# A hybrid encoder layer with product-key retrieval: half of the tokens' input projections moved from ahead of the gather loop into its slots 104 to 200

## The chip, the core and the metric

The kernel runs on one core of a Trainium2 chip. The metric is the device time of one execution in microseconds (us). The five engines are TensorE (PE), VectorE (DVE), ScalarE (ACT), GpSimd (POOL) and SyncE (SP); each works through its own list of instructions in order, and they meet through semaphores.

## The reference, cut to what matters

One layer for 512 prompt tokens and 32 sample tokens, D = 1024, everything in float32:

```
n    = rmsnorm(x)
proj = n @ w_in                      # qkv (3072), z, x_lru, y_lru, gate_a, gate_b (1024 each), beta, decay (16)
A    = gated DeltaNet(conv4+silu(qkv)), gated by silu(z)        # sequential over tokens, in chunks
B    = RG-LRU(conv4(x_lru)) * gelu(y_lru)                        # sequential over tokens
x    = x + (sigmoid(gate_a)*(A @ w_branch_a) + sigmoid(gate_b)*(B @ w_branch_b)) @ w_out
q    = rmsnorm(x) @ w_q;  8 heads x top-16 of 128x128 product keys -> 128 experts a token
x    = x + sum_k gelu(u_k . n) * gate_k * v_k                     # u, v: rows of two 16384 x 1024 tables
y    = rmsnorm(x)
```

The convolutions and both recurrences carry state from token to token, so later tokens need three rows of history and one hidden state from the earlier ones. The states and the last three pre-convolution rows are outputs too.

## The kernel before, in words

**Tokens and tiles.** Four prompt tiles of 128 tokens and a sample tile of 32. In the projections tokens lie along the free axis (544 columns, in two halves of 272) and features along the partitions. From the delta rule on, the work goes tile by tile.

**The front part.** `w_in` and `w_branch_b` arrive as 72 chunks of 128 output columns (512 KB each) in a ring of four buffers, in the order lx, ly, ga, gb, branch_b, z (8 each), qkv (24). Each chunk is split in two: ACT casts it to the rounded type fp32r (`split`, L919, into one of only two buffers `w_hi`), POOL subtracts to get the remainder (`lower`, L1190). The inputs were split likewise. PE (`quads`, L601) then runs hi x hi, lo x hi and hi x lo over 8 blocks of 128 and two column halves: 48 one-pass matmuls of 272 columns a chunk. ACT empties the banks (`evac` L888 to L894, or `through` L966) and then casts the chunk after the next one, which can't start before PE has left that `w_hi` buffer. DVE does the convolutions (`conv`, L1259 and L1263) and the LRU (L1277 to L1293); ACT its tanh, exp and square root (L983 to L991). The gates of the LRU are 16 small products (L638). What tiles 1 to 3 need later is written to DRAM (`spill`, 18 transfers) and read back a tile at a time (`loads`).

**The trunk.** For each tile `delta` (two groups of four heads, one stage apart) and `tail` (products with w_a, w_out, w_q and the keys, one 512 KB weight chunk to a stage, ordinary float32 matmuls) are generators that name the stage of each step. `BD` and `BT` hold the first stage of each tile's delta and tail: 47 stages (35 for a full tile's solve, 12 more) and 36. `Weave.to(stage)` emits all steps up to a stage into an engine's list, and every engine and SP use the same stages.

**The gather loop.** There are 544 slots, one expert per token row each: a slot fetches 128 rows of 8 KB (u and v side by side, 1.05 MB) by an indirect DMA (POOL, L1211) into a ring of 8 slot buffers. DVE forms the dot with u (`dot`, L1541), ACT its gelu once per pair of slots (L1170), DVE the share (L1550), ACT a diagonal matrix (L1156), and PE adds share times v to the token's sum in two PSUM banks (`add_row`, L863), three slots later (VLAG). POOL may fetch into a buffer again when PE has used it (`slot_free`). Between slots each engine does its share of the trunk: `stage_at` gives the stage reached at each slot, from a table:

```
PACE = [(2, 92, BD[1], BD[2]), (92, 220, BD[2], BD[3]), (220, 348, BD[3], stages)]
```

So tile 1's delta and tail lie in slots 2 to 92, tile 2's in 92 to 220, tile 3's and the sample tile's in 220 to 348; the rest has gathers alone. Tile 0's delta and tail come ahead of the loop. Tile t's slots begin at 128 t, and the picks of the experts (`pick_halves`, `pick_top`, `pick_experts` on DVE, one for 16 slots) run LAG = 2 blocks ahead.

## Time and profile before

| | us |
|---|---|
| runs (median of 3) | 2364.37 (2353.43 to 2369.49) |
| profiled execution, its own time | 2363.84 |
| its span, first to last instruction | 2361.7 |
| front part, first to last L601 matmul | 49.3 to 533.0 |
| delta and tail of tile 0, first pick | 533.0 to 702.4 |
| first dot of the gather loop | 711.7 |
| last dot | 2345.2 |
| mean granted TensorE clock | 0.948 |

The page gives each engine's busy time; a view by windows gives it for any stretch, with the granted clock (1.00 is 2.4 GHz, 0.50 is 1.2 GHz) and the DMA share. Dots leave two records each (the operation and the read of its accumulator), float32 matmuls two as well. Recorded times of PE overlap, so that the distance from start to start is what one costs.

### The profile page before, as it was taken

How to read it: one execution, taken by the hardware profiler on the slowest of the kernel's cores; microseconds unless marked ns; L12 is line 12 of the kernel's file. 1: busy time of each engine (PE TensorE's matmuls, PEld its weight loads, DVE VectorE, ACT ScalarE, POOL GpSimd, SP SyncE). 2: the span in 40 equal slices, each digit the busy share in tenths (PEclk: the TensorE clock that was granted, in tenths of full speed). 3: DMA queues.
4: the chain of work that ended last, by engine and by line, in shares of the span. 5: the costliest groups of instructions: out<-in, count | busy, mean ns of one | idle time of the engine just before them, and what ended most of it. 6: DMA issues, size and time to landing. Idle time of an engine off the chain costs nothing.

```text
span 2361.7 us, 26994 instructions
## 1 busy us (share of the span) xinstructions
PE 2028.3 (86%) x9678; PEld 1331.2 (56%) x9678; DVE 1432.4 (61%) x3375; ACT 710.1 (30%) x1768; POOL 815.7 (35%) x631
## 2 busy tenths in 40 slices
PE   5999799998867998999988889998999777777776
PEld 5988799997745654555554456654536222322321
DVE  2603802775238974678865658868646667676754
ACT  3454223443114240352341233352312122221221
POOL 3423334440003333334333333334222434444442
PEclk6999899997888999999999999999999999999999
DMA  3212223422368999999999998999889999999997
GB/s 114 90 62 71 91 87 112 146 91 76 111 218 324 349 366 418 413 379 364 390 383 419 406 400 309 356 334 396 345 322 363 385 387 412 401 418 397 381 401 295
DMA packets 129642, 695.82 MB, mean 295 GB/s; under 512 B 14608, under 2 KB 33456, under 8 KB 59136
## 3 DMA queue, kind: packets, MB, share of 16 engines
q0 software_dynamic: 78416, 570.57, 61.6%
q1 hardware_dynamic: 50496, 121.69, 14.6%
q10 hardware_dynamic: 624, 2.23, 0.2%
q8 instruction: 57, 0.93, 0.2%
q14 instruction: 49, 0.40, 0.0%
HBM read 680.31 MB, written 13.61 MB: 294 GB/s over the span
## 4 chain that ended last, share of the span: by engine, by line
PE 45%; DMA 23%; DVE 17%; issue 8%; ACT 3%; POOL 3%; SPq 1%; DVEq 0%; POOLq 0%; ACTq 0%
DMA arena<-in_uv,arena 19%; PE ps L863 18%; PE ps L601 12%; DVE arena L1541 6%; PE ps L784 4%; PE ps L808 2%; DMA arena<-in_w_out 2%; DMA arena<-in_w_a 2%; POOL w_lo L1190 2%; PE ps L735 1%; PE ps L734 1%; PE ps L725 1%; DVE i L1478 1%; ACT arena L1156 1%; DVE v L1475 1%
## 5 line engine op out<-in xcount | busy, mean ns | idle before, releaser
L863 PE MATMUL ps<-arena 128*128 128x512 f32 (+1 forms) x2176 | 1052.8, 622 | 222.2 <-ACT arena L1156 220.6
L1211 POOL DMA_INDIRECT arena<-in_uv,arena x544 | 611.7, 1125 | 1190.9 <-PE ps L863 987.9
L1541 DVE CUSTOM_DVE_ANT_0 arena<-arena 128x1024 f32<-128x1024 f32 x544 | 662.2, 1223 | 426.5 <-DMA arena<-in_uv,arena 420.8
L863 PEld LDWEIGHTS ps<-arena 128*128 128x128 f32 (+1 forms) x2176 | 390.8, 192 | 723.6 <-issue 392.2
L1170 ACT ACTIVATE gelu_d<-dots 128x2 f32<-128x2 f32 x272 | 55.4, 204 | 1057.7 <-DVE dots L1541 1050.5
L601 PE MATMUL ps<-n_hi,w_hi 128*128 128x272 f32 x1024 | 298.5, 292 | 8.2 <-POOL w_lo L1190 8.2
L601 PE MATMUL ps<-n_hi,w_lo 128*128 128x272 f32 x1024 | 299.4, 292 | 0.0
L601 PE MATMUL ps<-n_lo,w_hi 128*128 128x272 f32 x1024 | 297.4, 290 | 0.0
L1190 POOL TENSOR_TENSOR w_lo<-arena,w_hi 128x1024 fp32r<-128x1024 f32 x72 | 188.4, 2617 | 298.4 <-ACT w_hi L919 298.3
L601 PEld LDWEIGHTS ps<-n_hi,w_hi 128*128 128x128 f32 x1024 | 195.9, 191 | 9.0 <-issue 8.1
L601 PEld LDWEIGHTS ps<-n_lo,w_hi 128*128 128x128 f32 x1024 | 196.1, 191 | 0.0
L601 PEld LDWEIGHTS ps<-n_hi,w_lo 128*128 128x128 f32 x1024 | 195.4, 191 | 0.0
L1156 ACT ACTIVATE arena<-ident,share 128x128 f32<-128x128 f32 x512 | 173.6, 386 | 0.3
L784 PEld LDWEIGHTS ps<-arena 128*128 128x128 f32 x1024 | 135.0, 202 | 36.5 <-issue 21.0
L784 PE MATMUL ps<-arena 128*128 128x128 f32 (+1 forms) x1024 | 137.1, 292 | 10.2 <-DMA arena<-in_w_a 8.2
L1263 DVE SCALAR_TENSOR_TENSOR arena<-arena,dn_w 128x547 f32<-128x547 f32 x72 | 98.6, 1370 | 10.4 <-DVE arena L1259 0.2
L919 ACT CAST w_hi<-arena 128x1024 fp32r<-128x1024 f32 x72 | 76.1, 1058 | 53.7 <-PE ps L601 53.7
L735 PE MATMUL ps<-arena 128*128 128x128 f32 (+1 forms) x448 | 75.5, 265 | 0.0
L725 PEld LDWEIGHTS ps<-arena 128*128 128x128 f32 (+1 forms) x448 | 54.3, 187 | 33.8 <-issue 24.6
L808 PE MATMUL ps<-arena 128*128 128x512 f32 x128 | 65.8, 633 | 8.4 <-DMA arena<-in_w_out 8.1
L1170 ACT ACT_TABLE_LOAD x54 | 69.3, 1283 | 1.0
L734 PE MATMUL ps<-arena 128*128 128x128 f32 (+1 forms) x368 | 66.3, 267 | 0.0
(232 smaller groups left out, 2127.7 us busy)
## 6 DMA issues: line engine op xcount, KB each, us to landing
arena<-in_stream SPq DMA_DIRECT2D x72, 512.0 KB, 3.3
arena<-in_w_a SPq DMA_DIRECT2D x32, 512.0 KB
arena<-in_w_out SPq DMA_DIRECT2D x32, 512.0 KB
arena<-in_w_q SPq DMA_DIRECT2D x32, 512.0 KB
arena<-in_uv,arena POOLq DMA_INDIRECT x544
spill<-arena SPq DMA_DIRECT2D x12, 512.0 KB, 5.8
arena<-spill SPq DMA_DIRECT2D x4, 1536.0 KB, 11.6
spill<-arena SPq DMA_DIRECT2D x6, 640.0 KB, 7.5
```

Source lines behind the costliest of these rows:

```text
L601: mm = pe.matmul(ps[:, b + half, 0:HALF], w[:, k, :], rhs[:, k, cols], start=(k == 0 and w is w_hi[s % 2] and rhs is rhs_hi), stop=(k == K ...
L734: pe.matmul(bank(PA)[:, i, 0:L], tinvt[0:L, h, 0:L], pmat[0:L, h, 0:L], start=True, stop=True)
L735: mm = pe.matmul(bank(PC)[:, i, 0:L], pmat[0:L, h, 0:L], tinvt[0:L, h, 0:L], start=True, stop=True)
L784: mm = pe.matmul(ps[:, bank + j, at:at + N], w[:, k, :], rhs[:, k, 0:N], start=(k == 0), stop=(k == KC - 1))
L808: mm = pe.matmul(ps[:, 5 + half, :], mix[:, k, 0:P], w[:, cols], start=(k == 0), stop=(k == KC - 1))
L863: mm = pe.matmul(ps[0:L, half, :], diag[k % NDIAG][:, 0:L], ring[k % SLOTS][:, D + half * 512:D + (half + 1) * 512], start=False, stop=k % ...
L1156: act.activation(diag[k % NDIAG][:, 0:L], eye, ACT.Identity, scale=share[u % 4][:, k % 2:k % 2 + 1]).then_inc(diag_ready, 1)
L1170: act.activation(gelu_d[u % 4][:, :], dots[u % 4][:, :], ACT.Gelu).then_inc(gelu_ready, 1)
L1190: pool.tensor_tensor(w_lo[s][:, :, :], wring[s], w_hi[s % 2][:, :, :].bitcast(F32), ALU.subtract).then_inc(lo_ready, 1)
L1211: pool.indirect_dma_start(out=ring[kk % SLOTS], out_offset=None, in_=a["uv"], in_offset=bass.IndirectOffsetOnAxis(ap=idx[:, kk:kk + 1], ax ...
L1263: ins = dve.scalar_tensor_tensor(out=y[:, 0:CONVW], in0=x[:, k:k + CONVW], scalar=w[:, k:k + 1], in1=y[:, 0:CONVW], op0=ALU.mult, op1=ALU.add)
L1541: ins = dve.tensor_tensor_reduce(ring[s][:, 0:D], ring[s][:, 0:D], n2p if t == NTILE else n2[t % 2], 1.0, 0.0, ALU.mult, ALU.add, dots[k / ...
```

## The change

Tiles 0 and 1 (N1 = 256 columns) are projected up front, the other N2 = 288 tokens inside the gather loop. The normalised input of those goes to DRAM (`spill_n`) and comes back at slot 104 as `NG`, 294 columns wide (3 + 256 + 3 + 32: room for the history).

- **Up front**: still 72 chunks, each with 24 matmuls of 256 columns into one bank (four banks in rotation in place of two pairs). Convolutions, LRU, gates and activations on 256 columns; results go straight to tiles 0 and 1 in SBUF, so the 18 spills and the loads for tiles 1 and 2 are gone. The parameter of the first normalisation and the first four chunks are issued ahead of the other parameters.
- **In the loop**: two new generators, `second_sums` and `second_lru`, of 87 stages from BG on. The same 72 chunks and the two LRU gate matrices are read again (74 transfers of 512 KB, through the four `wslot` buffers that the tails use), and multiplied in ordinary float32 with 294 columns (branch_b 288), rotating over six banks; then history columns written into PSUM by ACT, convolutions by DVE straight from PSUM, the LRU for 288 tokens, activations into tile 2's place, and for tile 3 and the samples through three staging buffers (`stg`) to `spill3` by 48 transfers of 80 KB.
- **Pace**: tile 1 in slots 1 to 104, the second projections in 104 to 200, tile 2 in 200 to 239, tile 3 and samples in 239 to 367. LAG is 1 and a block's picks lie at its slots 1, 4 and 7 (before 3, 7, 11).
- **Every second expert in slots 104 to 238** (odd, and not in the first 11 of a tile: 62 of them) is added by DVE into `fin` with one 128x1024 operation; PE and the diagonal matrix on ACT are left out for it. At a tile's end DVE adds the two sums (`join`).

```diff
-        PICK_AT = (3, 7, 11)
-        LAG = 2
+        PICK_AT = (1, 4, 7)
+        LAG = 1
+        def on_dve(k):
+            return 104 <= k < 239 and k % P > 10 and k % 2 == 1
...
+            if u == 2:
+                BG = stages
+                stages += 87
+                feed += [("stream", CH_LX + n, BG + n) for n in range(KC)]
+                feed += [("gate", j, BG + 17) for j in range(2)]
+                for first, at in ((CH_GA, 18), (CH_Z, 26), (CH_LY, 34)):
+                    feed += [("stream", first + n, BG + at + n) for n in range(KC)]
+                for n in range(KC):
+                    feed += [("stream", CH_GB + n, BG + 44 + 2 * n), ("stream", CH_BB + n, BG + 45 + 2 * n)]
+                feed += [("stream", CH_QKV + m, BG + 60 + m) for m in range(3 * KC)]
...
-        PACE = [(2, 92, BD[1], BD[2]), (92, 220, BD[2], BD[3]), (220, 348, BD[3], stages)]
+        PACE = [(1, 104, BD[1], BG), (104, 200, BG, BD[2]), (200, 239, BD[2], BD[3]), (239, 367, BD[3], stages)]
...
 # PE, front part
-                        for half in range(2):
-                            cols = slice(half * HALF, (half + 1) * HALF)
-                            for k in range(KC):
-                                for w, rhs in ((w_hi[s % 2], rhs_hi), (w_hi[s % 2], rhs_lo), (w_lo[s], rhs_hi)):
-                                    mm = pe.matmul(ps[:, b + half, 0:HALF], w[:, k, :], rhs[:, k, cols],
+                        for k in range(KC):
+                            for w, rhs in ((w_hi[s % 2], rhs_hi), (w_hi[s % 2], rhs_lo), (w_lo[s], rhs_hi)):
+                                mm = pe.matmul(ps[:, s, 0:N1], w[:, k, :], rhs[:, k, :],
...
 # PE, in the loop
+            def second_sums():
+                def product(p, i, rhs, n):
+                    c = group_at(i)
+                    w = wslot[c % RING].rearrange("p (k n) -> p k n", n=P)
+                    pe.wait_ge(chunk_in[c % RING], landed(c))
+                    if p >= 6:
+                        pe.wait_ge(*freed(p - 6))
+                    for k in range(KC):
+                        mm = pe.matmul(ps[:, group_bank(p), 0:n], w[:, k, :], rhs[:, k, :],
+                                       start=(k == 0), stop=(k == KC - 1))
+                    mm.then_inc(tw_used, 1)
...
 # SP
+                yield BG
+                sp.wait_ge(sc_copied, 2)
+                sp.wait_ge(n_spilled, 16)
+                sp.dma_start(NG[:, :, HIST:HIST + N1], a["spill_n"][:, :, 0:N1]).then_inc(ng_in, 16)
+                sp.dma_start(NG[:, :, SMP0:NP2], a["spill_n"][:, :, N1:N2]).then_inc(ng_in, 16)
...
 # ACT: history into PSUM, and silu of the convolved columns
+                def halo(j, p, c):
+                    act.wait_ge(tw_used, group_done(c))
+                    x = ps[:, group_bank(p), :]
+                    act.copy(tails[:, j, :].rearrange("p (a n) -> p a n", a=2),
+                             x[:, N1:N1 + 2 * (HIST + TS)].rearrange("p (a n) -> p a n", a=2)[:, :, 0:HIST])
+                    act.copy(x[:, 0:HIST], hist1[:, j, :])
+                    old = lru_hist[:, j, :] if j < KC else dn_hist[:, j - KC, :]
+                    act.copy(x[:, HIST + N1:SMP0], old).then_inc(pad_ready, 1)
+                def silu(m):
+                    q = 3 * KC + m
+                    act.wait_ge(conv_ready, CONVS + KC + m + 1)
+                    act.wait_ge(stg_out[q % 3], uses(q // 3))
+                    y = yc[m % 2]
+                    act.activation(td[2][:, q, :], y[:, 0:P], ACT.Silu)
+                    act.activation(stg[q % 3][:, 0:P], y[:, P:N1], ACT.Silu)
+                    act.activation(stg[q % 3][:, P:P + TS], y[:, YS0:YS0 + TS], ACT.Silu).then_inc(conv_used, 1)
...
 # DVE: convolution from PSUM (one tensor_scalar, three of these), and an expert's row
+                    for k in range(1, CW):
+                            ins = dve.scalar_tensor_tensor(out=y[:, 0:n], in0=x[:, k:k + n], scalar=w[:, k:k + 1],
+                                                           in1=y[:, 0:n], op0=ALU.mult, op1=ALU.add)
+            def add_row(k):
+                t = k // P
+                v, w = ring[k % SLOTS][:, D:2 * D], share[k // 2 % 4][:, k % 2:k % 2 + 1]
+                dve.wait_ge(share_ready, k // 2 + 1)
...
+                    dve.wait_ge(row_added, k - on_pe(k))
+                    dve.scalar_tensor_tensor(out=fin, in0=v, scalar=w, in1=fin, op0=ALU.mult, op1=ALU.add
+                                             ).then_inc(row_added, 1)
```

## Rows read from the trace of the kernel before

**Rows 1.** The page, part 1: busy time of the engines.
```profile
PE 2028.3 (86%) x9678; PEld 1331.2 (56%) x9678; DVE 1432.4 (61%) x3375; ACT 710.1 (30%) x1768; POOL 815.7 (35%) x631
```

**Rows 2.** Windows by stretch: busy us (records) of each engine, granted clock, DMA share, GB/s.
```profile
49.30:533.00 483.70, 461.66 (x3524) 455.48 (x3522) 222.87 (x214) 180.71 (x376) 185.29 (x72) 0.97 0.29 92
533.00:620.50 87.50, 71.23 (x513) 68.46 (x512) 45.17 (x83) 32.62 (x82) 0.59 (x1) 0.85 0.15 51
620.50:702.40 81.90, 60.79 (x348) 48.80 (x348) 15.05 (x49) 7.05 (x10) 0.03 (x1) 0.85 0.64 218
...
711.70:1008.70 297.00, 269.04 (x1176) 165.91 (x1176) 208.23 (x539) 87.35 (x232) 104.87 (x88) 0.95 0.96 374
1008.70:1403.00 394.30, 347.64 (x1360) 198.76 (x1361) 280.40 (x738) 121.63 (x313) 143.27 (x129) 0.97 0.99 391
1403.00:1828.50 425.50, 400.94 (x1836) 228.64 (x1835) 295.75 (x798) 145.06 (x386) 139.66 (x126) 0.98 0.93 349
1828.50:2347.00 518.50, 386.23 (x799) 141.94 (x797) 339.99 (x902) 114.38 (x341) 216.70 (x194) 0.96 0.98 396
```

**Rows 3.** Windows of the dots (L1541) alone, two records each: DVE busy, clock, DMA.
```profile
711.70:1008.00 296.30, 111.30 (x182) 0.95 0.96 374
...
1828.00:2347.00 519.00, 240.15 (x392) 0.96 0.98 396
```

**Rows 4.** Chain of waits in order of time, the front part: start, us, what.
```profile
288.91 244.12 PE ps L601 x1920
```

**Rows 5.** Timeline of ACT and POOL between two chunks: start, us, what, idle before.
```profile
382.16 0.63 ACT L966 ACTIVATE arena<-ps 128x544 f32 x1 [4.48 <-PE ps L601]
...
382.69 1.04 ACT L919 CAST w_hi<-arena 128x1024 fp32r<-128x1024 f32 x1
...
383.80 2.39 POOL L1190 TENSOR_TENSOR w_lo<-arena,w_hi 128x1024 fp32r<-128x1024 f32 x1 [3.65 <-ACT w_hi L919]
```

**Rows 6.** Waits of PE between 49 and 533: us, times, longest.
```profile
PE ps L601 <- DVE b_lo L1293: 11.9, 1, 11.9
```

**Rows 7.** Timeline, the start: last parameter's issue by SP, first wait of DVE.
```profile
14.20 0.43 SPq L491 DMA_DIRECT2D dtb<-in_dn_dt_bias  x1
...
19.88 3.55 DVE L1230 RECIPROCAL arena<-arena 128x544 f32<-128x544 f32 x1 [18.75 <-DMA dtb<-in_dn_dt_bias]
```

**Rows 8.** Chain of waits, the tail of tile 0.
```profile
626.56 10.30 DMA arena<-in_w_a
...
651.93 8.61 DMA arena<-in_w_out
```

**Rows 9.** Chain of waits at 1708 and 1787: one expert's row, one 160-column weight chunk.
```profile
1708.36 1.72 PE ps L863 x4
...
1787.16 2.17 PE ps L784 x16
```

**Rows 10.** Groups by line, then one line's view, then the timeline, all of DVE.
```profile
L1541 DVE CUSTOM_DVE_ANT_0 arena<-arena 128x1024 f32<-128x1024 f32 x544 | 662.2, 1223 | 426.5 <-DMA arena<-in_uv,arena 420.8 <-issue 3.8
...
L1463 DVE SCALAR_TENSOR_TENSOR arena<-arena,rs x4: 1277/1279/1285, 665.6 to 1777.6; 128x1024 f32<-128x1024 f32 x4
...
63.32 0.79 DVE L1263 SCALAR_TENSOR_TENSOR arena<-arena,lru_w 128x547 f32<-128x547 f32 x1
```

**Rows 11.** Timeline of DVE: the first and the last instruction of one block's picks.
```profile
701.94 0.48 DVE L1475 MAX8 v<-arena 128x8 f32<-128x128 f32 x2
...
711.59 0.23 DVE L1531 TENSOR_SCALAR arena<-gexp,gsum 128x16 f32<-128x16 f32 x1
```

**Rows 12.** Timeline of ACT: a diagonal pair, then a change of function table.
```profile
724.56 0.68 ACT L1156 ACTIVATE arena<-ident,share 128x128 f32<-128x128 f32 x2
725.26 1.28 ACT L1031 ACT_TABLE_LOAD   x1
726.55 0.27 ACT L1031 ACTIVATE rqk<-ps,eps_col 128x8 f32<-128x8 f32 x1
```

**Rows 13.** Windows: four levels of tile 0's solve, one idle gap of PE in each.
```profile
577.00:602.40 25.40, 22.57 (x194) 21.74 (x192) 16.07 (x26) 5.18 (x9) 0.00 (x0) 1.00 0.01 2
```

More of the change, by code:

```diff
@@ L441, in trunk_program @@
                 stages += solved(NTILE) + 11
-            BT.append(stages)
+            b = stages
+            BT.append(b)
             stages += 36
+            feed += [("w_a", n, b + n) for n in range(KC)] + [("w_out", k, b + 8 + k) for k in range(KC)]
+            feed += [("g2", u, b + 20)] + [("w_q", n, b + 23 + n) for n in range(KC)] + [("keys", 0, b + 33)]
         FIRST = BD[1]
-        PACE = [(2, 92, BD[1], BD[2]), (92, 220, BD[2], BD[3]), (220, 348, BD[3], stages)]
+        PACE = [(1, 104, BD[1], BG), (104, 200, BG, BD[2]), (200, 239, BD[2], BD[3]), (239, 367, BD[3], stages)]
         def stage_at(kk):
@@ L466, in to, with trunk @@
                     self.at += 1
-        def trunk(delta, tail):
-            parts = []
+        def trunk(delta, tail, second):
+            parts = list(second)
             for u in range(NTILE):
@@ L565, in _ @@
-            flow = Weave([p for u in range(NTILE) for p in (weights(u), loads(u))])
-            flow.to(1)
-            spill(5, conv_used, CONVS)
+                        old, u, stage = feed[c - RING]
+                        yield stage
+                        if old == "g2":
+                            sp.wait_ge(n2_ready, norms(u))
+                        elif old == "gate":
+                            sp.wait_ge(g_gate_mm, 2 * KC)
+                        else:
+                            sp.wait_ge(tw_used, used_after(c - RING))
@@ new lines, in put, with spills @@
+            def put(q, row):
+                sp.dma_start(a["spill3"][:, row, :], stg[q % 3]).then_inc(stg_out[q % 3], 16)
+            def spills():
+                for q in range(2 * KC):
+                    yield BG + 19 + q
+                    sp.wait_ge(g_evac, q + 1)
+                    put(q, q if q < KC else KC + q)
+                    if q == 2 * KC - 1:
+                        sp.wait_ge(g_last, 1)
+                        sp.dma_start(o["lru_last"], lru_last[:, :, :]).then_inc(small_out, 16)
+                for n in range(KC):
+                    yield BG + 46 + 2 * n
+                    sp.wait_ge(g_bb, n + 1)
+                    put(2 * KC + n, KC + n)
+                for m in range(3 * KC):
+                    yield BG + 63 + m
+                    sp.wait_ge(conv_used, 3 * KC + m + 1)
+                    put(3 * KC + m, 3 * KC + m)
+                sp.wait_ge(pad_ready, 2 * CONVS)
+                sp.dma_start(o["tails"], tails[:, :, :]).then_inc(small_out, 16)
@@ L568, in _ @@
+            flow = Weave([loads(), weights(), spills()])
             flow.to(FIRST)
@@ L1568, in _ @@
             for kk in range(NS + VLAG + 6):
+                t, k = ends(kk)
+                if k == VLAG and mixed(t):
+                    join(t)
                 if kk < NS:
```

661 lines of the change are left out of this document (452 added, 209 removed).

## The prediction, made before the change was run

> **What bounds the kernel now.** I read the windows first, cut where the kernel changes its work. The front part, 483.7 us, is PE's: 462 busy at clock 0.97 with DMA at 0.29 [rows 2], and in the chain of waits 1920 matmuls follow one another for 244.12 us, 0.127 us each [rows 4]. Delta and tail of tile 0 follow, 87.5 and 81.9 us, with no gathers beside them. Then the loop: 297, 394.3, 425.5 and 518.5 us for 91, 129, 128 and 196 dots [rows 2, 3]. The last stretch has gathers alone and is DMA's: 2.65 us a slot, DMA share 0.98, PE busy 386 of 518. A slot moves 1.05 MB, so 396 GB/s is the loop's rate. The third stretch is PE's, 401 busy of 425.5. PE is 86% busy over the whole span [rows 1], yet for another reason in each stretch, so each is costed by itself.
>
> The sums run against the profiled execution: span 2361.7, own time 2363.84 (2.1 around the span), 0.5 below the median 2364.37 of the runs. About 1% is what a measurement can tell here, so faster means under 2341 and slower over 2388.
>
> **Term 1, up to the first dot (now 711.7).**
> Start: the first reciprocal waited until 19.88 for the last parameter, and SP's queue reached that at 14.20 [rows 7]. With its own parameter early it can start near 14.2, and the subtractions on POOL beside it halve. I take 7 us. The other parameters now land behind 2 MB of weights; the 8 normalisations, unchanged in width, cover that. Both directions are small: -7, bounds -3 and -9.
>
> A chunk: 24 matmuls in place of 48. At 0.127 us each that is 3.05 us; in proportion to 256 of 272 columns it would be 2.9. PE no longer sets the pace, because `w_hi` has two buffers: when PE leaves chunk c, ACT empties the bank and casts c+2, POOL subtracts, and only then can PE start. From 382.16, where PE's end releases ACT, to 386.19, where POOL ends, that takes 4.03 us [rows 5]. It was hidden behind the 6.05 us of the chunk between; now it isn't. With an eviction of 0.28 rather than 0.53 it is 3.8; the two semaphores at its ends, not in these rows, I put at 0.2 and PE's own chunk with its last result at 3.15, together 7.15 us for two chunks, 3.57 each; where DVE works beside POOL I add 0.1 to 0.3 (two history copies shrink to one). 72 x 3.65 = 263 us. The Trainium skill ("TensorE: Matmul & The Clock Gate", back-to-back issue gap) gives N/2.4 + 2.5 ns, 109 ns for 256 columns and 116 for 272. The trace has 127 for 272, so the row stands; by the page the front would be 72 x 0.2 = 14 us shorter.
>
> Beside the chunks: LRU gates 10 (16 us on 544 columns), tanh and exp ahead of ga's third chunk 6, square roots 4, the scans ahead of branch_b 2 where 11.9 us were waited [rows 6], half clock at first 5: 27 us. So the products run from 42 to 332, 201 earlier than before; bounds 185 and 215.
>
> From there to the first dot it was 178.7 us. The tail waited 10.3 and 8.6 us for w_a and w_out [rows 8], behind 3 MB of tile 1's data that SP now doesn't fetch: -15. One block of picks fewer ahead of the first dot, 9.9 us of which the landing of the first rows hides half: -5 [rows 11]. The last convolution is shorter: -2. First dot at 332 + 156.5 = **488**.
>
> **Term 2, slots 0 to 104 (tile 1).** 297 us for 92 slots, 12 more at 2.65 (32), less 3 MB of loads for tile 2 (8): **321**. The picks move from slots 3, 7, 11 to 1, 4, 7 one block ahead; POOL wants the index near slot 11, so three slots cover them. With that cover gone each block would stall for the few us of a pick.
>
> **Term 3, slots 104 to 200, the woven projections.**
> PE: a weight chunk of 160 columns takes 2.17 us in 16 records and an expert's row 1.72 in four of 512 columns [rows 9], both 0.84 ns a column and record. So 294 columns cost 3.95 a chunk: 64 x 3.95 + 8 x 3.87 = 284, gates 8. 41 of 96 rows go to DVE: 55 x 1.72 = 95. Together 386.
> DMA: 96 x 1.05 + 74 x 0.52 + 5 MB for `NG` and the staged tile = 145 MB, 365 us at 396 GB/s.
> DVE: 96 dots x 1.22 = 117, shares 8, 41 additions x 1.28 = 52 [rows 10], six picks x 9.9 = 59, LRU and products 26. A convolution was one operation at about 0.5 and three at 0.79 for 547 columns when POOL was quiet [rows 10]; for 291 from PSUM I take 0.5 each, 2.05 with its waits, 66 for 32. Together 328. No row has this form; 0.42 in proportion and 0.75 (a PSUM start cost as large as the scaled operation) bound it, 305 to 355.
> ACT: history, activations, 55 diagonals and up to 96 changes of table at 1.28 [rows 12]: some 250. The Trainium skill ("ScalarE: Activation LUTs", what ACT_TABLE_LOAD costs) gives 2.66 us a change, of which 1.38 is a drain. Here the load starts 0.02 after the operation before it and the next follows 0.01 behind it, so no drain is seen. By the page ACT would come to 382, level with PE, and the stretch to the 470 of the third rival.
> POOL only issues gathers (143 busy of 394 in a like stretch). SP's queue takes 74 weight loads, 48 staging writes and two loads of `NG`; at 0.43 an issue [rows 7] 53 us, covered. What is queued behind its waits are the weights, four chunks (16 us) ahead.
> PE is the longest. The PE-bound stretch before took 6% more than PE's busy time [rows 2]; the first load of `NG`, for which PE stands still with the gathers behind it, makes it 7%: **413**, bounds 386 and 470.
>
> **Term 4, slots 200 to 239, tile 2's delta and tail.** 83 stages in 39 slots, 2.1 a slot where there was 0.65 to 0.9. Delta takes 22 of these slots, and alone it needed 87.5 us with PE 71 and DVE 45 busy [rows 2]. The gather adds 57 us to DVE (22 dots, 11 additions, 1.4 picks, shares) and 19 to PE (11 rows). If all overlaps, DVE's 102 sets the end; if all is serial, 163. The two head groups let one engine work for one group while another gathers, as in slots 0 to 92, where delta was hidden; a gather still cuts into the chain every second stage. I take 122, a third of the way. The tail, 17 slots: PE 63 (48 for the products, 15 for rows), DMA 35 MB or 89 us, less what ring and weight buffers hold at its start: 80. **202**, bounds 166 and 255.
>
> **Term 5, the rest.** Tile 3 with the samples in 128 slots as before, 425.5; 177 slots at 2.65, 469; end 14.7. The tile's reads are the same. `join` adds 1.3 us twice, and the copies by ACT that it replaces took as long: nothing.
>
> **Sum.** 488 + 321 + 413 + 202 + 425.5 + 469 + 14.7 = 2333, plus 2.1: **2335 us**, 1.2% below. 223 us are won ahead of the loop; inside it terms 3 and 4 cost 615 us for 135 slots that at 2.65 would take 358, while before they paid for tile 2 with some 50 over that rate.
>
> **Rivals.**
> *The loop hides it (0.18): 2250.* If only bytes and the busiest engine count, term 3 is 390, term 4 166, term 2 310 and the front ends 10 earlier: 2335 - 23 - 36 - 11 - 10 = 2255. For: DMA holds 0.97 to 0.99 over whole stretches of woven work [rows 2]. Against: 1403 to 1828 fell to 0.93, with 1 stage a slot.
> *Everything is given back (0.26): 2364.* Term 4 at 220 and term 3 at 425 are enough. For: both are estimates with one-sided risks. Against: nothing but their size.
> *In slots 104 to 200 DVE takes turns with PE (0.19): 2400, slower.* In the qkv part a slot has on DVE a dot 1.22, half an addition 0.64, 0.9 of a convolution 1.9, picks and share 0.7, in all 4.4 us, and on PE 0.86 + 3.6 = 4.5. Neither has slack. A pick of 3 us in one slot can't be caught up, PE stands for the diagonal behind it and POOL for the buffer. At 4.9 us a slot term 3 is 470 and, with term 4 pushed to 210, the time 2400; it is slower by 1% from about 466. Against: the ring lets DVE be some slots ahead.
> *The front runs at 1.2 GHz (0.05): 2405.* PE now idles in every chunk; at that level 24 matmuls take 5.1 us, the pair 9.2, 72 chunks 72 us more. Against: at 577 to 602 PE had such a gap every 6 us at clock 1.00 [rows 13].
>
> **Chances and range.** The forecast has 0.32; its own range is 2300 to 2365, and 0.24 of it lies under 2341. Faster by over 1% is that 0.24, the first rival's 0.18 and 0.03 of the second: 0.45. Within 1% are 0.08 of the forecast and 0.21 of the second: 0.29. Slower are 0.02 of the second, 0.19 and 0.05: 0.26. The range takes in the bounds of terms 3 and 4 without their joint extremes: 2250 to 2420.
>
> **What would show it.** The first dot near 488, and 3.6 us from one chunk to the next in the front with waits of PE for POOL's w_lo, where now there are none to speak of. Dots at 104 to 200 spaced 4.3 us, PE 90% busy there. In slots 200 to 239 spacing over 5 us with DMA under 0.9. The prediction is wrong in its front if chunks follow at 3.0 or above 4.5; in its middle if DMA is above 0.95 in slots 104 to 239.

## The result, and the profile after

| | before | after |
|---|---|---|
| median of the runs taken together, us | 2364.84 (4 runs) | 2391.31 (4 runs, 2380.31 to 2399.94) |
| ratio to before, 95% interval | | 1.0117 [1.0062, 1.0172] |
| profiled execution, its own time | 2363.84 | 2391.45 |
| its span | 2361.7 | 2389.6 |

The change makes the kernel 1.2% slower; the forecast was 1.2% faster. The windows of the kernel after, cut at its own marks: the products of the front part, delta and tail of tile 0, then from the first dot the slots 0 to 104, 104 to 200, 200 to 239, 239 to 367 and 367 to 543. They answer to [rows 2]; the columns are the same.

```profile
core 0: us, PE busy (x) PEld busy (x) DVE busy (x) ACT busy (x) POOL busy (x), PEclk, DMA share, GB/s
41.70:363.00 321.30, 246.67 (x1764) 237.83 (x1763) 166.77 (x203) 135.12 (x245) 170.10 (x71) 0.90 0.35 113
363.00:447.00 84.00, 70.38 (x515) 67.48 (x513) 44.25 (x84) 31.60 (x77) 0.00 (x0) 0.87 0.07 26
447.00:514.50 67.50, 54.50 (x345) 45.16 (x344) 11.89 (x36) 6.84 (x9) 0.00 (x0) 0.90 0.64 210
524.00:847.40 323.40, 294.11 (x1233) 177.59 (x1234) 236.73 (x624) 98.82 (x259) 123.01 (x104) 0.95 0.98 384
847.40:1276.80 429.40, 397.50 (x1412) 269.37 (x1411) 316.62 (x714) 206.25 (x486) 113.44 (x97) 0.97 0.92 344
1276.80:1483.30 206.50, 156.57 (x863) 117.63 (x862) 135.12 (x282) 54.38 (x129) 44.23 (x38) 0.87 0.69 261
1483.30:1905.30 422.00, 401.40 (x1883) 230.84 (x1884) 298.15 (x801) 142.10 (x386) 146.67 (x127) 0.99 0.94 358
1905.30:2373.00 467.70, 359.46 (x722) 131.36 (x721) 313.52 (x844) 106.36 (x308) 198.44 (x175) 0.93 0.99 397
```

The reader is to see one row above all, the first. In [rows 2] PE was 95% busy (462 of 483.7) at clock 0.97; now it is 77% busy (247 of 321) at 0.90. 483.7 became 321.3, where the forecast had 290. Against the sum of the prediction, term by term (the last column is the row above less the forecast):

| | forecast | measured | off by |
|---|---|---|---|
| term 1, first dot | 488 | 524.0 | +36 |
| of it, the front's products | 290 | 321.3 | +31 |
| term 2, slots 0 to 104 | 321 | 323.4 | +2 |
| term 3, slots 104 to 200 | 413 | 429.4 | +16 |
| term 4, slots 200 to 239 | 202 | 206.5 | +5 |
| term 5, slots 239 to the end | 909.2 | 906.3 (with an end of 16.5) | -3 |

Together +56, which is the 2389.6 of the span against the 2333 of the sum. Ahead of the loop 188 us were won (711.7 to 524.0), and the loop gave back 216: its 544 slots took 1634 us before (dot 0 to dot 543) and 1849 now.

What PE waited for in the front of the kernel after (us, times, longest). It answers to [rows 6], whose wait for `b_lo` came first in the kernel before, ahead of one for `w_lo`:

```profile
PE ps L702 <- POOL w_lo L1432: 60.8, 35, 7.9
PE ps L702 <- DVE b_lo L1536: 12.0, 1, 12.0
PE ps L738 <- ACT arena L1123: 1.7, 1, 1.7
```

The second wait of the kernel before, between 49 and 533:

```profile
PE ps L601 <- POOL w_lo L1190: 8.2, 3, 5.9
```

The timeline of ACT and POOL in a group of the front without convolutions (branch_b), with one start of PE between them. It answers to [rows 5]:

```profile
207.53 1.05 ACT L1054 CAST w_hi<-arena 128x1024 fp32r<-128x1024 f32 x1 [15.66 <-PE ps L702]
...
210.33 1.05 ACT L1054 CAST w_hi<-arena 128x1024 fp32r<-128x1024 f32 x1 [1.75 <-PE ps L702]
...
211.18 0.38 PE L702 MATMUL ps<-b_hi,w_hi 128*128 128x256 f32 x1 [0.89 <-POOL w_lo L1432]
211.45 2.40 POOL L1432 TENSOR_TENSOR w_lo<-arena,w_hi 128x1024 fp32r<-128x1024 f32 x1 [0.40 <-ACT w_hi L1054]
...
214.43 1.05 ACT L1054 CAST w_hi<-arena 128x1024 fp32r<-128x1024 f32 x1 [3.06 <-PE ps L702]
```

From the first cast to the third 6.9 us pass, two chunks: the handshake that the prediction had put at 7.15. One chunk follows at 3.0 us, the next only at 3.9 (4.2 in the other groups), because it waits for its subtraction. PE's own pace is the distance between the starts of its matmuls: 296.88, 297.00, 297.12 and so on, 0.12 us each, 2.9 for the 24 of a chunk.

### The profile page after: what moved, and what is told of

Read it like the earlier page. It is cut to its first block, busy times and chain, and to the rows that moved or that the text cites. A ratio compares the mean times of both kernels' runs of the same rounds, so it can differ in the third digit from the quotient of the medians.

```text
span 2389.6 us, 26031 instructions
## 1 busy us (share of the span) xinstructions
PE 2012.5 (84%) x8854; PEld 1301.0 (54%) x8854; DVE 1541.8 (65%) x3618; ACT 801.4 (34%) x1930; POOL 813.8 (34%) x629
## 4 chain that ended last, share of the span: by engine, by line
PE 45%; DMA 19%; DVE 17%; issue 9%; POOL 5%; ACT 5%; DVEq 0%; POOLq 0%; SPq 0%; ACTq 0%
PE ps L1010 20%; DMA arena<-in_uv,arena 15%; PE ps L958 11%; DVE arena L1872 5%; POOL w_lo L1432 4%; PE ps L885 4%; DVE arena L1509 2%; PE ps L909 2%; PE ps L826 1%; DMA arena<-in_w_a 1%; DMA spill<-arena 1%; PE ps L836 1%; DVE arena L1502 1%; PE ps L835 1%; ACT arena L1398 1%
## 5 line engine op out<-in xcount | busy, mean ns | idle before, releaser
L1010 PE MATMUL ps<-arena 128*128 128x512 f32 (+1 forms) x1928 | 948.0, 629 | 165.3 <-ACT arena L1398 164.4
L1412 ACT ACTIVATE gelu_d<-dots 128x2 f32<-128x2 f32 x272 | 55.4, 204 | 936.8 <-DVE dots L1872 936.0
L958 PE MATMUL ps<-arena 128*128 128x294 f32 (+1 forms) x1152 | 295.2, 412 | 14.3 <-DMA arena<-spill_n 14.3
L958 PEld LDWEIGHTS ps<-arena 128*128 128x128 f32 x1152 | 219.8, 191 | 99.4 <-issue 38.7
L702 PE MATMUL ps<-n_hi,w_hi 128*128 128x256 f32 x512 | 158.7, 310 | 58.3 <-POOL w_lo L1432 58.2
L1398 ACT ACTIVATE arena<-ident,share 128x128 f32<-128x128 f32 x450 | 155.6, 386 | 0.3 <-issue 0.2
L702 PE MATMUL ps<-n_lo,w_hi 128*128 128x256 f32 x512 | 154.1, 301 | 0.0
L702 PE MATMUL ps<-n_hi,w_lo 128*128 128x256 f32 x512 | 153.7, 300 | 0.0
L885 PEld LDWEIGHTS ps<-arena 128*128 128x128 f32 x1024 | 130.0, 197 | 34.7 <-issue 14.5
L702 PEld LDWEIGHTS ps<-n_hi,w_hi 128*128 128x128 f32 x512 | 107.6, 210 | 65.2 <-issue 41.4
L702 PEld LDWEIGHTS ps<-n_lo,w_hi 128*128 128x128 f32 x512 | 108.1, 211 | 0.0
L702 PEld LDWEIGHTS ps<-n_hi,w_lo 128*128 128x128 f32 x512 | 107.7, 210 | 0.0
L1894 DVE SCALAR_TENSOR_TENSOR arena<-arena,share 128x1024 f32<-128x1024 f32 x60 | 77.1, 1285 | 2.1
```

Source lines behind the costliest of these rows:

```text
L702: mm = pe.matmul(ps[:, s, 0:N1], w[:, k, :], rhs[:, k, :], start=(k == 0 and w is w_hi[s % 2] and rhs is rhs_hi), stop=(k == KC - 1 and w ...
L885: mm = pe.matmul(ps[:, bank + j, at:at + N], w[:, k, :], rhs[:, k, 0:N], start=(k == 0), stop=(k == KC - 1))
L958: mm = pe.matmul(ps[:, group_bank(p), 0:n], w[:, k, :], rhs[:, k, :], start=(k == 0), stop=(k == KC - 1))
L1010: mm = pe.matmul(ps[0:L, half, :], diag[on_pe(k) % NDIAG][:, 0:L], ring[k % SLOTS][:, D + half * 512:D + (half + 1) * 512], start=False, s ...
L1398: act.activation(diag[n % NDIAG][:, 0:L], eye, ACT.Identity, scale=share[u % 4][:, k % 2:k % 2 + 1]).then_inc(diag_ready, 1)
L1412: act.activation(gelu_d[u % 4][:, :], dots[u % 4][:, :], ACT.Gelu).then_inc(gelu_ready, 1)
```

## The experiments

All ratios are to the kernel before, run beside the experiment on the same chip. "First dot" and the stages are read from the profiled execution.

### hi4: four buffers for `w_hi`

The cast of a chunk and its subtraction may run ahead of PE, so that neither waits for it.

```diff
-        w_hi = [rounded(f"w_hi{s}", WHI + s * KC * P, KC, P) for s in range(2)]
+        w_hi = [rounded(f"w_hi{s}", at, KC, P) for s, at in enumerate((WHI, WHI + KC * P, STATE + 2 * D, STATE + 3 * D))]
...
-                act.copy(w_hi[c % 2][:, :, :], wring[slot]).then_inc(hi_ready, 1)
+                act.copy(w_hi[c % 4][:, :, :], wring[slot]).then_inc(hi_ready, 1)
...
-                        evac(j, j + (pr0 - first), s, first > 0 or not first_quad or s > 1)
                         if s < splits:
                             split(s + 2, i + (ch0 - first) // RING)
+                        evac(j, j + (pr0 - first), s, first > 0 or not first_quad or s > 1)
...
```

(`split(s + 2, ...)` is now issued ahead of the eviction; PE and POOL take `w_hi[s]`.)

> The changed kernel with four buffers of rounded weights in place of two, and each cast issued ahead of the eviction before it, so that PE no longer waits for the chain eviction, cast, subtraction. Theory A (the front part lost 31 us on the forecast because PE idles 60.8 us for the subtraction in 35 waits, and each idle stretch lets its clock fall to 1.2 GHz): the chunks follow at 2.9 us, the half-clock pieces in the front mostly go, the front part (321 us) shrinks to 250 to 270, the whole kernel by 50 to 70 us to about 2330. Rival B (the subtraction on POOL and the casts set the pace themselves, or DVE and POOL slow each other once both run without pause): front 300 or more, total above 2370.

Measured: 2372.9 us, ratio 1.0046 [1.0023, 1.007]. That is 0.7% below the ratio of the change, 17 us; the first dot came 26.4 us earlier (497.6). Neither expectation was met as a whole: the front's products took 293 us (41.7 to 335.2), more than the 250 to 270 of theory A and less than the 300 of rival B, and the total lies just above B's 2370. Some 10 of the 26 us were lost again in slots 239 to 367 of the profiled execution (432.9 us at clock 0.97, for 422.0 at 0.99), which the edit doesn't touch. A window of its front where nothing is convolved (branch_b and z), columns as above:

```profile
204.00:240.00 36.00, 35.76 (x298) 35.56 (x298) 2.12 (x5) 19.71 (x24) 29.31 (x13) 1.00 0.56 186
```

A window of hi4 in the qkv group:

```profile
262.00:304.00 42.00, 32.19 (x241) 30.41 (x241) 37.80 (x40) 16.56 (x40) 23.63 (x10) 0.97 0.37 123
```

The same window of the kernel after:

```profile
262.00:304.00 42.00, 32.96 (x265) 31.77 (x263) 31.08 (x33) 18.80 (x42) 26.10 (x11) 1.00 0.44 139
```

Where nothing is convolved, PE is now busy throughout (35.76 of 36) and a chunk takes 2.9 us. Where DVE convolves, nothing is gained: 241 matmuls in the 42 us, where the kernel after has 265, and DVE is busy for 37.8 of them. Behind the bound of the two buffers lay another. The timeline of DVE and POOL in that group of hi4 shows it:

```profile
289.89 0.34 DVE L1502 TENSOR_SCALAR arena<-arena,dn_w 128x256 f32<-128x256 f32 x1
290.38 3.83 DVE L1509 SCALAR_TENSOR_TENSOR arena<-arena,dn_w 128x256 f32<-128x256 f32 x3
291.56 2.37 POOL L1432 TENSOR_TENSOR w_lo<-arena,w_hi 128x1024 fp32r<-128x1024 f32 x1 [1.87 <-ACT w_hi L1054]
294.13 0.34 DVE L1502 TENSOR_SCALAR arena<-arena,dn_w 128x256 f32<-128x256 f32 x1
```

The three operations of a convolution take 3.83 us, and POOL's subtraction of 2.37 lies inside that time. From 289.89 to 294.13 is 4.24 us, the pace of the group, and DVE stands idle for hardly any of it. 3.83 less 2.37 leaves 1.46, half a microsecond an operation. Taken one by one, the first two operations take 0.48 us each; the third, which starts 0.08 us after POOL's subtraction and ends 0.28 us after it, has all of the rest:

```profile
291.01 0.48 DVE L1509 SCALAR_TENSOR_TENSOR arena<-arena,dn_w 128x256 f32<-128x256 f32 x1
...
291.64 2.57 DVE L1509 SCALAR_TENSOR_TENSOR arena<-arena,dn_w 128x256 f32<-128x256 f32 x1
```

The other wait grew: PE stood 18.4 us for `b_lo` in hi4, where the kernel after had 12.0, because PE now came to branch_b sooner.

### all_pe, half_k and dve367: who sets slots 104 to 200, and 239 to 367

all_pe gives the rows of slots 104 to 238 back to PE; dve367 puts every second row on DVE up to slot 366; half_k leaves out half of each woven product.

```diff
-            return 104 <= k < 239 and k % P > 10 and k % 2 == 1
+            return False                                              # all_pe
...
-            return 104 <= k < 239 and k % P > 10 and k % 2 == 1
+            return 104 <= k < 367 and k % P > 10 and k % 2 == 1       # dve367
...
-                    for k in range(KC):
+                    for k in range(KC // 2):                          # half_k, the woven products
```

> The changed kernel without additions by DVE: every expert's row goes through PE. Theory A (slots 104 to 200 are PE's): 41 rows more at 1.72 us make that stretch 429 + 55 to 70, slots 200 to 239 little longer (PE has room, 159 busy of 209), total 2391 + 60 to 85. Rival B (DVE and PE take turns there; DVE's 52 us of additions cost as much as they save): the same or up to 20 us faster.

Measured: 2436.01 us, ratio 1.0313 [1.0262, 1.0365]; slots 104 to 200 took 484.8 us with PE 465.3 busy and DMA at 0.86. 41 rows on PE in that stretch cost 55.4 us, 1.35 each, as theory A had it (55 to 70). The whole grew by 45 us and not by 60 to 85, because slots 200 to 239 fell by 10 us (206.5 to 196.6): there the rows are better on PE. The rows on DVE are worth 45 us of execution time in all.

> The changed kernel with only the first four of eight blocks in each product of the woven projections (half of the sum is left out); weight transfers, history, convolutions and all else stay. It takes 142 us from PE in slots 104 to 200. Theory A (PE sets that stretch): it falls from 429 us until DMA's 365 or DVE's 317 hold it, to 365 to 385. Rival B (in-order turns between DVE, ACT and PE): it stays above 405.

Measured: 2344.37 us in a single execution. The window of its slots 104 to 200:

```profile
847.40:1235.50 388.10, 286.86 (x845) 168.74 (x844) 315.56 (x714) 206.04 (x489) 106.01 (x97) 0.89 0.95 381
```

PE loses 110.6 us of work, the stage only 41.3, to 3 us above the 365 to 385 of theory A. DMA is nearly full there, at 0.95 and 381 GB/s, so that little is left to win in this stage by taking more from PE: some 20 us, an estimate (0.05 of 388). PE now waits 60.9 us for the diagonals of ACT, 20.5 for weights and 13.2 for `NG`, and its clock was 0.89; which of these held the last 3 us isn't shown.

> The changed kernel with DVE adding every second row up to slot 366 in place of 238, 59 rows more. Slots 239 to 367 have PE busy 399 of 419 us, DVE 296. If that stretch is PE's (theory A) it falls to DMA's 365 to 390, total 2391 - 25 to -50. Rival B (the additions lengthen the turns of DVE as much as they relieve PE): total within 10 us of 2391.

Measured: 2404.83 us, ratio 1.0192 [1.0138, 1.0246]. That is 0.7% above the ratio of the change, with intervals that overlap: no gain, where theory A had 25 to 50 us, and 13.5 us above the change by the times, where rival B had at most 10. The window of its slots 239 to 367, then what PE waited for in it:

```profile
1482.00:1910.00 428.00, 343.38 (x1633) 205.69 (x1635) 368.64 (x859) 124.25 (x326) 146.13 (x129) 0.88 0.92 352
```
```profile
PE ps L1010 <- ACT arena L1398: 57.9, 32, 5.3
```

The same wait in the kernel after, in the same slots:

```profile
PE ps L1010 <- ACT arena L1398: 17.0, 18, 2.4
```

PE has 58 us less to do than in the kernel after (343 in place of 401), and the stretch is no shorter. DVE is now the longest, at 369, and PE waits for it by way of ACT's diagonals (L1398), 57.9 us for 17.0. With these gaps PE's clock fell too, to 0.88 where the kernel after had 0.99, so that part of the 343 is slow work. Both engines sit in the path of a slot, and relieving PE by loading DVE won nothing here; how much of that the waits did and how much the clock, this run does not separate.

### narrow: does DVE hold back slots 104 to 200?

The convolution steps inside the loop write 8 columns; the others are left out.

```diff
-                            ins = dve.scalar_tensor_tensor(out=y[:, 0:n], in0=x[:, k:k + n], scalar=w[:, k:k + 1],
-                                                           in1=y[:, 0:n], op0=ALU.mult, op1=ALU.add)
+                            ins = dve.scalar_tensor_tensor(out=y[:, 0:8], in0=x[:, k:k + 8], scalar=w[:, k:k + 1],
+                                                           in1=y[:, 0:8], op0=ALU.mult, op1=ALU.add)
```

> The changed kernel in which the convolution steps that DVE runs inside the gather loop, in slots 104 to 200, write 8 columns instead of about 290 (the rest of those columns is left out; TensorE's work, the expert rows on DVE, the evictions and the transfers stay as they are). Question: do DVE's convolutions, beside its rows, lengthen slots 104 to 200 (429.4 us, with TensorE busy 397.5 and DVE 316.6)? Theory 'TensorE sets this stage': 429.4 becomes 419 to 429, since TensorE waited only where the convolutions of the first groups come together (some 10 us) and has the same work. Rival 'DVE and TensorE take turns here': each us off DVE shows in part; DVE loses 60 us or more of its 316, and the stage becomes 405 or less. Whole execution about 2382 under the theory, 2365 or less under the rival.

Measured: 2385.77 us in a single execution; slots 104 to 200 took 426.3 us (429.4 in the kernel after). A window of that stretch, narrow:

```profile
841.70:1270.00 428.30, 399.87 (x1416) 270.46 (x1415) 293.77 (x718) 209.11 (x491) 107.58 (x98) 0.97 0.92 345
```

DVE is relieved of only 23 us (316.6 to 293.8), not the 60 that I had reckoned with. The group of these steps says why:

```profile
L1736 DVE SCALAR_TENSOR_TENSOR arena<-ps,dn_w,arena 128x8 f32<-128x8 f32 x72 | 16.3, 226 | 2.5
```

A step of 8 columns still takes 226 ns, where one of 291 takes 522. So the test is weaker than it was meant to be. Of the 23 us the stage shows 3, and 426.3 lies in the theory's 419 to 429: as far as a relief of 23 us can tell, DVE does not set it.

### subs: the qkv subtractions on DVE

With four `w_hi` buffers, and DVE subtracting the qkv chunks itself, between its convolutions.

```diff
-            lower(0, CH_BA)
+            lower(0, CH_QKV)
...
+            def lower(c):
+                dve.wait_ge(hi_ready, c + 1)
+                dve.tensor_tensor(w_lo[c % RING][:, :, :], wring[c % RING], w_hi[c % RING][:, :, :].bitcast(F32),
+                                  ALU.subtract).then_inc(lo_dve, 1)
...
+            for m in range(3 * KC):
+                if m + 2 < 3 * KC:
+                    lower(CH_QKV + m + 2)
+                conv(N_LX + m, dn_w[:, m, :], m % 2, m > 1)
```

> hi4 with the subtractions of the 24 qkv chunks moved from POOL to DVE, between its convolutions. In hi4 the qkv chunks follow at 4.22 us though PE needs 2.9: DVE's three operations of a convolution take 3.83 us, and POOL's subtraction of 2.37 lies inside them. Theory A (DVE and POOL take turns at one resource, so that their times add): with 1.1 us of subtraction on DVE and POOL still, a convolution operation is back at about 0.45, the chunks follow at 2.95 to 3.1, total 25 to 31 us below hi4. Rival B (the handshake ACT, DVE, ACT sets the 4.22): within 5 us of hi4, or slower by DVE's extra work (26 us).

Measured: 2341.0 us, ratio 0.9908 [0.9878, 0.9939], 1.4% below hi4 and 32 us by the times, where theory A had 25 to 31; rival B is refuted. The first dot came at 469.1, and the 24 qkv chunks took 69.3 us, for 94.9 in hi4. Timeline of DVE in its qkv group:

```profile
284.10 1.22 DVE L1556 TENSOR_TENSOR w_lo<-arena,w_hi 128x1024 fp32r<-128x1024 f32 x1
...
285.24 0.35 DVE L1504 TENSOR_SCALAR arena<-arena,dn_w 128x256 f32<-128x256 f32 x1
...
285.62 1.52 DVE L1511 SCALAR_TENSOR_TENSOR arena<-arena,dn_w 128x256 f32<-128x256 f32 x3
```

The window that answers to those of hi4 and of the kernel after:

```profile
262.00:304.00 42.00, 42.00 (x352) 42.00 (x351) 40.47 (x72) 25.20 (x58) 0.00 (x0) 1.00 0.56 186
```

The same three operations take 1.52 us. DVE has one operation more, of 1.22, and is still quicker through a chunk: 2.9 us in place of 4.24. More work on the busier engine removed the bound. That DVE stands while POOL subtracts, and does not merely run slower beside it, is what the durations say: 3.83 is 1.52 + 2.37, less 0.06, and in hi4 the whole of it fell on the one operation that lay beside POOL's. The Trainium skill ("SBUF — State Buffer", "SBUF: two separate sides") says the same of two engines that share one pair of ports: the pair is a lock held for a whole instruction, and a VectorE operation with two SBUF inputs against a GpSimd operation that reads SBUF is a case of it; the trace agrees.

### zfirst, zfirst98, zfirst_d197: what the first two left

zfirst is subs with the z group ahead of branch_b, so that PE has 8 chunks to do while DVE ends the scans. zfirst98 moves the marks of the woven work from 104 and 200 to 99 and 190. zfirst_d197 is zfirst with DVE's rows ending at slot 196.

```diff
-GROUP_CHUNKS = {"lx": KC, "ly": KC, "ga": KC, "gb": KC, "branch_b": KC, "z": KC, "qkv": 3 * KC}
+GROUP_CHUNKS = {"lx": KC, "ly": KC, "ga": KC, "gb": KC, "z": KC, "branch_b": KC, "qkv": 3 * KC}
...
-        PACE = [(1, 104, BD[1], BG), (104, 200, BG, BD[2]), (200, 239, BD[2], BD[3]), (239, 367, BD[3], stages)]
+        PACE = [(1, 99, BD[1], BG), (99, 190, BG, BD[2]), (190, 239, BD[2], BD[3]), (239, 367, BD[3], stages)]  # zfirst98
...
-            return 104 <= k < 239 and k % P > 10 and k % 2 == 1
+            return 104 <= k < 197 and k % P > 10 and k % 2 == 1       # zfirst_d197
```

> subs with the z chunks ahead of branch_b, so that the LRU's scans on DVE lie beside z's products. PE now stands 18.4 us for the last scan in hi4. Expected 15 to 20 us below subs if that wait only goes; nothing if PE then waits elsewhere for the same scans.

Measured: 2336.0 us, ratio 0.9885 [0.9848, 0.9922]. The first dot came at 466.4, 2.7 us before that of subs, of the 15 to 20 expected; the intervals of subs and zfirst overlap. The wait for `b_lo` went from 18.4 to 10.6 us only, although PE had eight chunks, 23 us, to do meanwhile: the scans ended at 206.7 in place of 191.1. POOL's subtractions for z now lay beside them. Two of the same DVE operations in zfirst, one beside POOL's subtractions (the four in the first line) and one after them:

```profile
187.43 10.36 POOL L1433 TENSOR_TENSOR w_lo<-arena,w_hi 128x1024 fp32r<-128x1024 f32 x4 [1.43 <-ACT w_hi L1055]
...
193.13 2.44 DVE L1537 TENSOR_TENSOR b_lo<-arena,b_hi  x1
...
206.25 0.42 DVE L1537 TENSOR_TENSOR b_lo<-arena,b_hi  x1
```

In the LRU's last part, six operations for each of its 8 blocks up to `b_lo`, 18 operations of DVE were held up like that, 36 us together over the shortest of their kind; in subs they were 10, with 20 us. So the same standstill that subs removed for the convolutions lengthens the scans, and new work for POOL beside them took back most of what the order of the groups gave.

> zfirst with the pace changed: tile 1 in slots 1 to 99, the woven projections in 99 to 190, tile 2 in 190 to 239 (49 slots in place of 39). Theory A (tile 2's stretch is bound by the latency of its chain, PE 76% and DMA 69% busy, so more gathers fit beside it at nearly no cost, while slots 104 to 200 are PE's by their content): tile 2's stretch grows by less than 15 us, the two before it lose 10 slots, 26 to 30 us: total 10 to 20 us below zfirst. Rival B (the gathers are serial to the chain, 5.3 us a slot wherever they lie): within 5 us of zfirst.

Measured: 2334.33 us, ratio 0.9893 [0.9852, 0.9934]: not to be told from zfirst, as rival B had it.

> zfirst with additions by DVE only in slots 104 to 196, not in tile 2's stretch. Without any additions by DVE that stretch took 196.6 us against 206.5. Theory A (there DVE's work lies on the chain and PE has room): 5 to 10 us faster than zfirst. Rival B: no change, as the additions there lie beside PE's waits.

Measured: 2326.76 us, ratio 0.9861 [0.9833, 0.989], 9 us under zfirst where theory A had 5 to 10; its slowest execution (2329.22) is faster than the fastest of zfirst (2334.46), though the intervals of the ratios overlap. The profiled execution is its fastest, 2316.91. Its windows of slots 104 to 200 and 200 to 239:

```profile
785.20:1211.30 426.10, 394.61 (x1407) 267.73 (x1406) 315.63 (x714) 205.91 (x486) 109.85 (x96) 0.97 0.92 345
1211.30:1410.80 199.50, 177.52 (x949) 126.93 (x948) 111.02 (x264) 60.75 (x148) 42.46 (x37) 0.94 0.74 272
```

In slots 200 to 239 PE has 21 us more work than in the kernel after (177.5 for 156.6), DVE 24 less, and the stage is 7 us shorter, while the clock went from 0.87 to 0.94. In zfirst itself the stage took 210.1 us at 0.84. all_pe agrees (196.6 us there). The rows of this stage belonged on PE.

### lx_d197 and lx_98_d187: the lx subtractions as well

lx_d197 is zfirst_d197 with DVE subtracting the eight lx chunks too. lx_98_d187 is lx_d197 with the woven work in slots 99 to 190 and DVE's rows in 99 to 186.

```diff
-            quads(0, CH_GA, 0, n_hi, n_lo)
+            quads(0, CH_LY, 0, n_hi, n_lo, lo_dve, 0)
+            quads(CH_LY, CH_GA, 0, n_hi, n_lo, lo_ready, CH_LY)
...
-            lower(0, CH_QKV)
+            lower(CH_LY, CH_QKV)
```

> zfirst_d197 with the subtractions of the lx chunks (the first 8) moved from POOL to DVE as those of the qkv chunks are. Theory, as shown by subs for qkv: with POOL's subtraction out of the way a convolution row of three operations takes about 1.5 us instead of 3.8, so that a chunk takes about 2.96 us instead of 4.22: 8 x 1.26 = 10 us less in the front, first dot at 452 instead of 462.3, and the time 2317 instead of 2327. Rival 'the first chunks are paced by the loading of their weights': the lx chunks are the first ones, and their weights come by DMA while the last load is under way; then the front starts no sooner and gains 0 to 3 us, time 2325.

Measured: 2318.8 us, ratio 0.9826 [0.9791, 0.9862]. The front's window:

```profile
41.30:296.00 254.70, 225.24 (x1763) 222.31 (x1762) 165.97 (x235) 146.74 (x253) 98.86 (x41) 0.93 0.43 143
```

254.7 us, where zfirst_d197 had 262.4: 8 of the 10 us that were reckoned, with the wait for `b_lo` 1.3 us longer (12.5 for 11.2). The first dot came 5 us earlier, at 457.3; the other 3 us were lost between the last product and the first dot. The median is 8 us lower, but the intervals of lx_d197 and zfirst_d197 overlap.

> lx_d197 with the woven work starting at slot 99 instead of 104, its middle mark at 190 instead of 200, and the expert rows on DVE in slots 99 to 186. The work is the same; what changes is how TensorE's woven products and DVE's rows lie against the stretch of slots 200 to 239, which in the changed kernel is cheap (206 us for 39 slots, 5.3 each) against 4.5 for a slot with alternate rows on DVE. Theory: TensorE is the bound in all of it, so that moving marks only moves the stages: within 8 us of lx_d197. Rival: with rows returned to TensorE ten slots earlier its load rises by 10/2 rows of about 1.7 us, 8 us more. Which of the two is the best version is not told apart in advance; 2310 to 2325.

Measured: 2331.05 us (2307.3 to 2336.66), ratio 0.9851 [0.9783, 0.992]. The median lies outside the 2310 to 2325 expected and 12 us above lx_d197, but one execution is the fastest of all; the interval holds that of lx_d197, so neither theory is settled. lx_d197 is the best version that was shown: 1.7% faster than the kernel before, 2.9% than the changed one.

## Why the prediction was wrong

**The step that failed is the front part of term 1**: "The products run from 42 to 332". They ran from 41.7 to 363.0, within 0.3 of the start and 31 past the end; 363 is also past the bound of the term (533 less 185, 348). From there to the first dot it was 161.0 us, for a forecast of 156.5. The chunks can be read from the first matmul of each. At full clock a pair takes 7.2 us (4.2 and 3.0), as forecast. What came on top:

- *The half clock*, put at 5 us. The clock of 0.90 over 321.3 us means 64 us at the lower level (2 x 0.10 x 321.3); in [rows 2] it was 0.97 over 483.7, 29 us. A pair of chunks that holds such a piece takes about 9.9 us (5.5 and 4.5, later 5.3 and 4.5); some nine of them make 25 us, 20 more than forecast. One piece, as a window:

```profile
165.70:169.10 3.40, 2.96 (x14) 2.97 (x15) 3.14 (x3) 0.00 (x0) 2.82 (x2) 0.50 0.00 0
```

  At this level its matmuls start 0.213 us apart, so that 16 would fit into 3.4 us; at full clock, at 0.12, 28. The fourth rival had the mechanism, at 72 us and a chance of 0.05, and I dismissed it by [rows 13], a stretch with one gap every 6 us. Here there was one every 7.2, and the clock fell again and again. In hi4, where PE had no gaps in the groups without convolutions, it was 1.00; but it was 1.00 as well in the window 262 to 304 of the kernel after, with PE 33.0 of 42 busy, while the same group fell to 1.2 GHz four times after it. And in hi4's qkv group it was 1.00 for 72 us with a gap in nearly every chunk and PE busy for 75%:

```profile
265.00:337.00 72.00, 53.95 (x418) 50.61 (x417) 64.19 (x71) 28.27 (x70) 38.86 (x17) 1.00 0.34 112
```

  So gaps go with the falls in these traces, but not every gap brings one; what decides it these runs do not show.
- *The scans ahead of branch_b*, put at 2 us because [rows 6] had 11.9 for twice the columns. It stayed 12.0, and the chunk with it took 15.1 us, some 11 more than its neighbours: 9 more than forecast. The scans themselves stood for POOL: eight of their operations took 2.2 to 2.6 us in place of 0.3 to 0.7, 15.5 us together, more than the wait (in the kernel before also eight, 16.9 us). The wait was not a matter of columns, then, and it did not shrink with them. No run takes POOL's work away there, so that this is read from the durations and not shown by a removal.
- *The convolutions beside POOL*, put at 0.1 to 0.3. The 8 chunks of lx followed at 4.2 each and not at 3.6, 5 us. In the qkv group the handshake of 7.2 hid it (DVE 31.1 of 42 busy), and it came out when hi4 removed that: most of the 24 chunks came at 4.2 where 2.9 were to be had, 26 us together, which subs then gained. I had priced the operation from [rows 10], at a moment when POOL was quiet, and PE's 6.05 us a chunk had hidden the rest.

Together 34 (an estimate from the chunks, as two of the slow ones in lx lie in pieces of half clock as well), less some 3 for a pair at 7.2 where the sum had 7.3.

What was right there is the handshake of two `w_hi` buffers: forecast 7.15 us for two chunks, measured 6.9 to 7.2 at full clock, and PE waits for POOL's `w_lo` in 35 places, as was to be seen. hi4 shows it by its removal. PE's own step was 0.120 us for 256 columns, where [rows 4] has 0.127 for 272: in proportion to the columns, 0.47 ns each. I had kept 0.127, which made a chunk 0.17 us too long. By the rule that the prediction cites from the Trainium skill ("TensorE: Matmul & The Clock Gate", back-to-back issue gap) it would be 109 ns. The rows do not agree, and they stand; that section gives the rule for matmuls alone, and here each has a weight load beside it.

**Term 3 was mis-sized by 16 us: 11.5 in PE's busy time and 5 in its idle part.** The prices of its sum hold: two chunks in 7.85 us in the chain of waits (forecast 7.9), a row in 1.72, an operation from PSUM in 0.522 (forecast 0.5), DVE's 316.6 (328). The chain of waits in the qkv part of the kernel after:

```profile
1099.78 7.85 PE ps L958 x32
1107.63 1.72 PE ps L1010 x4
```

The group of the convolution steps there:

```profile
L1736 DVE SCALAR_TENSOR_TENSOR arena<-ps,dn_w,arena 128x291 f32<-128x291 f32 x72 | 37.6, 522 | 2.5
```

PE's work came to 397.5, not 386, and around it 31.9 us were idle, against the 27 of my 7%. The waits of PE in this stretch say where:

```profile
PE ps L1010 <- ACT arena L1398: 16.8, 6, 5.9
PE ps L958 <- DMA arena<-spill_n: 14.3, 1, 14.3
```

The load of `NG` alone takes 14.3, where the forecast had put the seventh per cent, 4 us. The 11.5 more of busy time include the half clock: 0.97 over the stretch, some 26 us at the lower level. PE stood waiting for `NG` in 12 of them, so that the half clock cost some 7, an estimate (half of the other 14). Another 3 are the gates (8.9 us for 8) and some 2 us of matmuls that the sum left out. all_pe and half_k show that PE sets the stage, with DMA close behind; narrow took too little from DVE to rule it out altogether, but found nothing. The third rival (DVE takes turns with PE, 470) did not happen. Nor did a table change cost what the Trainium skill ("ScalarE: Activation LUTs", what ACT_TABLE_LOAD costs) gives for it: 96 loads of 1.283 us lie in the stretch with no drain to be seen, and ACT was busy 206 of 429.

**Terms 2, 4 and 5 hold**, to +2, +5 and -3. In term 4 a third of the way between full overlap and none was close (119.0 us for delta's 22 slots, forecast 122; 87.5 for the tail's 17, forecast 80): 5.3 us a slot with DMA at 0.69, as forecast "over 5 us with DMA under 0.9". That third was a guess, and the sum had neither the clock of 0.87 nor the 10 us that DVE's rows cost there. The first rival (bytes and the busiest engine alone) is refuted by that row.

**And the sign.** The third rival (2400) and the fourth (2405) have the nearest times. The third had it by luck: its term 3 of 470 was 429, and the front's 36 us, which it didn't have, made up for it. Of the fourth, the half clock did come, for 64 us of the front and not for all of it. The second, everything given back, gave the loss to terms 3 and 4; there it was 21 us, and the front's 36 turned a gain into a loss. The loop gave back 216 us, for a forecast of 195; the front brought 188 of 223. Four buffers, the subtractions of the convolved chunks on DVE, z ahead of branch_b and the rows of slots 197 to 238 back on PE turned 1.0117 into 0.9826, though what z and the lx chunks each gave lies within the noise. The front that the change left behind had its casts and subtractions placed for chunks of 6 us and was to run chunks of 3. No run gives the kernel before the same repairs. Its PE stood idle for only 22 of the 484 us of its front, 8.2 of them for `w_lo`, so that they have less to win there; but that the whole 1.7% is owed to moving the products is not shown.

## What to carry to other kernels

When the work of the bounding engine is halved, each chain beside it that took more than half of its old time comes out: price each by its own durations, for the engines as they will then overlap, not as they ran before. An operation's duration read where its neighbour was idle is a lower bound. Here VectorE's operations on two SBUF tensors stood still for nearly the whole of a GpSimd subtraction that they met, so that moving the subtraction onto VectorE shortened both. The profile counts the standstill as busy time, which makes VectorE look loaded where it is held up. And a gap that comes to the bounding engine costs more than its length where the granted clock falls behind it, which it did here for some gaps and not for others.

## What the runs showed of the hardware

- Three VectorE operations on 256 columns took 3.83 us (0.48 + 0.48 + 2.57 and what lies between) around one of GpSimd's of 2.37 in hi4, and 1.52 without it in subs. The same subtraction (128x1024) takes VectorE 1.22 us.
- It is not only operations with two inputs: the cast to `b_hi` on VectorE, with one, took 0.29 us alone and 2.27 beside a GpSimd subtraction (hi4, at 179.57 and 160.48), and a scan 0.69 and 2.84.
- TensorE at 77% busy in the front was granted 0.90 of its clock, falling to 1.2 GHz for short pieces, while a stretch of the same front with the same gaps (33.0 busy of 42) stayed at 1.00, and so did 72 us of hi4 at 75% busy.
- A convolution step that starts from PSUM took 226 ns for 8 columns (narrow) and 522 for 291 (the kernel after): by these two 1.05 ns a column and some 220 fixed.
